# Four late weight blocks and the low-part copies placed elsewhere in the routing stage of a two-layer decoder trunk

## The reference

```
h = RMSNorm(x) * (1 + scale2) + shift2
q = (h @ w_q) -> (256 tokens, 8 heads, 2 halves, 128)
s1, s2 = q[:, :, 0] @ key1.T, q[:, :, 1] @ key2.T      # 128 scores each
v1, i1 = top_k(s1, 16); v2, i2 = top_k(s2, 16)
top, sel = top_k(v1[:, None] + v2[None, :], 16)        # of 256 candidates
expert = (i1, i2) at sel; gate = softmax(top)
out = sum over (head, k) of gate * gelu(h . u[expert]) * v[expert]
x = x + (1 + gate2) * out
```

## Time and profile before

| | us |
|---|---|
| median of three runs | 2905.32 |
| lowest, highest | 2900.86, 2907.9 |
| the profiled execution, as timed | 2900.86 |
| its span in the profile | 2899.1 |
| PE busy in it | 2784.7 |
| DVE busy in it | 2244.3 |
| ACT busy, POOL busy | 1164.6, 576.4 |
| mean granted clock of TensorE | 0.991 of 2.4 GHz |

### The profile page before, as it was taken

How to read it: one execution, slowest core, us unless ns; L and a number is a source line. 1 busy time by engine, 2 the same in 40 slices (tenths; PEclk the granted TensorE clock), 3 DMA queues, 4 the chain that set the end, 5 groups by cost and what they waited for, 6 DMA issues and landing times. The chain is left out here.

```text
span 2899.1 us, 49831 instructions
## 1 busy us (share of the span) xinstructions
PE 2784.7 (96%) x19146; PEld 2528.6 (87%) x19146; DVE 2244.3 (77%) x4294; ACT 1164.6 (40%) x1662; POOL 576.4 (20%) x354
## 2 busy tenths in 40 slices
PE   6999998899999999999999999889999999999998
PEld 6998887789999998877899987777999999977776
DVE  7998665569987658888889987655899776688887
ACT  4534421234454444333355342222444444433334
POOL 0000002101677730000000000021207777200000
PEclk9999999999999999999999999999999999999999
DMA  7553442255788778788645535341568787788885
GB/s 290 189 188 121 162 162 74 89 204 189 211 236 258 198 221 288 277 287 288 244 155 189 175 109 192 100 153 41 215 206 225 230 244 200 245 289 290 284 278 198
DMA packets 258979, 593.71 MB, mean 205 GB/s; under 512 B 82608, under 2 KB 198064, under 8 KB 200240
## 3 DMA queue, kind: packets, MB, share of 16 engines
q1 hardware_dynamic: 205456, 573.53, 57.2%
q0 software_dynamic: 36864, 0.15, 2.6%
q10 hardware_dynamic: 16416, 16.78, 1.7%
HBM read 537.27 MB, written 53.08 MB: 204 GB/s over the span
## 5 line engine op out<-in xcount | busy, mean ns | idle before, releaser
L1067 PE MATMUL ps<-h_hi,u_hi 128*128 128x256 f32 x2048 | 588.2, 287 | 7.0 <-DVE u_lo L1931 6.4
L1067 PE MATMUL ps<-h_lo,u_hi 128*128 128x256 f32 x2048 | 579.2, 283 | 0.0
L1067 PE MATMUL ps<-h_hi,u_lo 128*128 128x256 f32 x2048 | 579.1, 283 | 0.0
L2175 POOL DMA_INDIRECT gate_rows<-route x256 | 474.8, 1854 | 300.0 <-DVE route L2045 132.0
L1931 DVE TENSOR_TENSOR u_lo<-ring,u_hi 128x1024 fp32r<-128x1024 f32 x256 | 312.3, 1220 | 200.3 <-ACT u_hi L1364 179.1
L1067 PEld LDWEIGHTS ps<-h_hi,u_hi 128*128 128x128 f32 x2048 | 392.3, 192 | 11.8 <-DVE u_lo L1931 11.5
L1067 PEld LDWEIGHTS ps<-h_lo,u_hi 128*128 128x128 f32 x2048 | 392.7, 192 | 0.0
L1067 PEld LDWEIGHTS ps<-h_hi,u_lo 128*128 128x128 f32 x2048 | 392.3, 192 | 0.0
L1385 ACT ACTIVATE u_hi<-ring 128x1024 fp32r<-128x1024 f32 x192 | 203.9, 1062 | 323.6 <-PE ps L1088 323.6
L1938 DVE TENSOR_TENSOR u_lo<-ring,u_hi 128x1024 fp32r<-128x1024 f32 x192 | 234.9, 1224 | 51.1 <-ACT u_hi L1385 50.8
L1364 ACT ACTIVATE u_hi<-ring 128x1024 fp32r<-128x1024 f32 x256 | 269.6, 1053 | 0.0
(11 more groups left out here) (374 smaller groups left out, 5290.8 us busy)
## 6 DMA issues: line engine op xcount, KB each, us to landing
ring<-in_stream SPq DMA_DIRECT2D x456, 1024.0 KB, 7.6
act_rows<-region SPq DMA_DIRECT2D x256, 128.0 KB
gate_rows<-rstd ACTq DMA_DIRECT2D x2, 8192.0 KB, 26.2
region<-gate_rows SPq DMA_DIRECT2D x256, 64.0 KB, 3.9
region<-act_rows SPq DMA_DIRECT2D x128, 128.0 KB, 4.5
small_inverse<-act_rows SPq DMA_DIRECT2D x128, 128.0 KB, 4.2
gate_rows<-route POOLq DMA_INDIRECT x256
region<-in_c SPq DMA_DIRECT2D x7, 512.0 KB, 5.6
```

What stands on the lines that cost most here:

```text
L1067: ins = mm(ps[:, c % 4, 0:T], x, y[:, k, :], start=k == 0 and i == 0, stop=k == KD - 1 and i == 2)
L2175: gp.indirect_dma_start(gate_cells, bass.IndirectOffsetOnAxis(ap=gate_at[:, r:r + 1].bitcast(I32), axis=0), gate_weight[:, r:r + 1], None, ...
```

## The change

It moves work and computes the same.

- `GATE_AFTER` is (13, 15, 17, 19) and was (30, 33, 36, 39): the four late blocks of `W_ada` come behind the U blocks of chunks 27, 31, 35 and 39, and no longer behind those of chunks 61, 67, 73 and 79. `gate_ada(j)` moves with them, from the loop over one-hot steps into `between`: it follows the `u_low` of the block's second chunk at once.
- `LO_IN_HEAD[1]` is (0, 0, 0, 0, 0, 0, 0, 2) and was (0, 0, 0, 0, 0, 1, 2, 3): the selections of the first pass hold two copies, both in the last head, instead of six.
- So every later count falls by four: `TOP_AT` is (37, 0) for (41, 6), `ROUTE_AT` is 47 for 51 and `GATE_AT` is 50 for 54. The `u_low` copies that are no longer in the routing come behind it.
- `portion` rounds down: three copies in a selection come behind steps 3, 6 and 9, and came behind steps 2, 5 and 8.

```diff
-GATE_AFTER = (30, 33, 36, 39)
+GATE_AFTER = (13, 15, 17, 19)
...
-LO_IN_HEAD = ((3,) * 8, (0, 0, 0, 0, 0, 1, 2, 3))
+LO_IN_HEAD = ((3,) * 8, (0, 0, 0, 0, 0, 0, 0, 2))
 LO_IN_TAIL = 11
-TOP_AT = (sum(LO_IN_HEAD[0]) + sum(LO_IN_HEAD[1]) + LO_IN_TAIL, sum(LO_IN_HEAD[1]))
+TOP_AT = (sum(LO_IN_HEAD[0]) + sum(LO_IN_HEAD[1]) + LO_IN_TAIL, 0)
...
 def portion(n, i, parts):
 
-    def upto(k):
-        return (2 * n * k + parts) // (2 * parts)
-    return upto(i + 1) - upto(i)
+    return n * (i + 1) // parts - n * i // parts
...
                     for c in range(split, split + n):
                         u_low(c)
+                        if c in (2 * p + 1 for p in GATE_AFTER):
+                            gate_ada(GATE_AFTER.index(c // 2))
                     split += n
...
                     if c + 2 < CHUNKS:
                         u_low(c + 2)
-                    if c + 1 in (2 * p for p in GATE_AFTER):
-                        gate_ada(GATE_AFTER.index((c + 1) // 2))
```

## The result

The changed kernel takes 2939.39 us (median of 4 runs, 2938.31 to 2944.91); the kernel before took 2904.74 in the same comparison (4 runs, 2900.86 to 2907.90). The ratio is 1.0117, with a 95% interval of 1.0103 to 1.0132: about 34 us slower. The prediction said 2932 with a range of 2915 to 2943 and called it slower. The direction, the range and the mechanism held; the size was 7 us too small against this median. The profiled execution took 2942.32 us, with a span of 2940.5.

The account below looks back on a forecast made before the run. PE was taken to bound most stages, with DVE leading in the second pass. Layer 2's +14.6 and layer 1's +13.2 made +27.8 us: 2928.7 on the profiled execution, 2933.1 on the median; forecast 2932, range 2915 to 2943.

Parts of the forecast that it names:

- Step 1: Ahead of chunk 0: the first u_low copy comes late, so PE waits 9.5 us.
- Step 2: At chunk 0: PE resumes at half clock for 4.2 us, chunk 0 lasts 2.1 us longer, net cost 1.4 us.
- The prediction's last sentence: If the clock stays at 1.00 at chunk 0, 1.4 us fall away, but decode(1) and the second pass give most back.
- Step 3: decode(1), ahead of the second pass: takes 32.5 us instead of 33.8, leaving PE a lead of 0.6 us at chunk 13.
- Step 4: Second pass of selections: three gate_ada add 6.9 us on DVE; chunk 36 starts 13.8 us later in layer 2.
- step 5: decode(0), behind the second pass: gate_ada(3) and two small instructions cost 1.8 us in layer 2, 1.0 in layer 1.
- step 6: One-hot loop: taking out the four gate_ada saves 1.0 us in layer 2, nothing in layer 1.
- Hidden gate_ada: Second pass and decode(0): DVE's added work is covered, so +12 us in all, 2917; chance 0.13.
- late loads: W_ada blocks sharing the ring with U blocks delay stores, 11 us a layer on top, 2954; chance 0.10.
- no difference: Whole kernel: PE's late start is absorbed, leaving the time within 0.3% (8.7 us); chance 0.03.
- faster: End of the U pass: DVE's routing, not PE, sets it; up to 11 us less in two layers, 2894; chance 0.03.

Follow-up runs that it names:

- PE kept busy: The changed kernel with 72 matmuls added on PE ahead of chunk 0, their results unused; 2936.43 us, ratio 1.0094 to the kernel before.
- experiments on gate_ada: The kernel before with only the four late W_ada blocks and their gate_ada moved early (GATE_AFTER 13, 15, 17, 19); 2925.57 us, ratio 1.0056.
- DVE's time alone: The kernel before with eight unused product-and-sum instructions a layer on DVE behind the copies of chunks 27, 31, 35 and 39, no load moved; 2925.54 us, ratio 1.0053.
- the later runs of the kernel before: 45 runs of the unchanged kernel before, on the two chips of the follow-up experiments; medians 2909.80 and 2910.58 us.

## Why the prediction came out as it did

*Step 1, the first copy.* Forecast: 9.5 us of idle. Measured: 9.53 and 9.54. Chunk 0 starts 10.66 us behind the last key scores, forecast 10.4. The counting of selections in the timeline was enough for this.

*Step 2, half clock.* Right: the granted clock is 0.50 (1.2 GHz) at 2151.50 to 2155.50, and chunk 0 takes 2156.83 - 2151.54 = 5.29 us, 5.0 by the forecast. PE kept busy showed the net price. It was 1.9 and 2.0 us at chunk 1, for 1.4 forecast, and 0.7 and 2.1 at the end of the stretches. Their sum is the 2.8 forecast (twice 1.4), but the layers differ by 1.4 us, so that agreement is in part luck. The prediction's last sentence, that steps 3 and 4 give most of it back, did not come true by chunk 36: 1.7 and 1.4 us were left there.

*Step 3, decode(1).* This is the mis-sized term of layer 2. It starts 13.9 us behind the landmark, as forecast (13.8), but takes 2188.26 - 2154.78 = 33.5 us, not 32.5. I had credited one microsecond to table loads that moved out of it; that credit was not there, and the row of before (33.8) was the better value. PE's lead at chunk 13 was as small as forecast: the copy ended at 2191.2, PE started it at 2191.7.

*Step 4, the second pass.* Forecast: 69.7 + 6.9 = 76.6 us, measured 2265.16 - 2188.26 = 76.9. The waits behind chunks 27, 31 and 35 came as said, 2.0 to 2.1 us for 2.2, but for the third of layer 1 (0.67). At chunk 36 layer 2 was 124.4 us behind the landmark and had been 109.2 before: +15.2 for 13.8 forecast, of which 1.0 is step 3. Layer 1 gave +11.9 for 12.2. The argument that a PE that takes chunks as DVE delivers them has no slack, in spite of its higher busy share, is what the experiments on gate_ada and on DVE's time alone bear out.

*The Trainium skill's rule.* By the highest occupancy (the Trainium skill, Perfetto Trace Analysis, Identifying the Most-Contended Engine) PE was the bound of that pass, and the rival that follows from it was priced at 2917. The trace after and these two experiments speak against that use of it where two engines are both nearly full.

*Steps 5 and 6, behind chunk 36.* From chunk 36 to the V pass, before took 2520.60 - 2224.85 = 295.75 us, after 2562.20 - 2265.30 = 296.90: +1.2 in layer 2, where 1.8 - 1.0 = 0.8 was forecast, and in layer 1 +2.4 for 1.0. Chunk 47, the last of decode(0) in the changed kernel, tells the two steps apart. In layer 2 it starts at 2256.68 before and 2299.18 after, in layer 1 at 830.85 and at 848.65. Up to there the delay grows by 2.1 and 1.9 us: step 5 was too small, by little in layer 2 (1.8) and by 0.9 in layer 1, where I had charged 1.0. Behind it layer 2 wins 0.9 us, the 1.0 of step 6, and layer 1 loses 0.5. So the size of step 6 held in layer 2, by luck: the largest wait of before behind this chunk, 0.58 us at chunk 51, was one for a copy of decode(0) and not in the one-hot loop. "In the one-hot loop, no wait at all" was wrong: where the kernel before waits 0.47 us for `hot` at chunk 66, the one after waits 0.87 at chunk 54, with no gate_ada left in that loop. The chains of waits lead both back to a store of a gelu result: 8.45 us long before, and after

```profile
2310.26 7.11 DMA act_rows<-region
```

The store ends at 2317.37, and high part, copy and one-hot matrices follow it up to PE's start at 2321.66. Reading the wait before as one for gate_ada was a mistake.

*What no step had.* Behind two microseconds of idle the clock was lower in some places: 0.60 at 2266.00 and 0.57 at 802.00, 24 and 23 matmuls in 4 us in place of 35 or 36. Each costs 11 or 12 x 0.12 = 1.3 to 1.4 us at the spot. Behind it the next wait for DVE is shorter by about as much (0.67 us at 814.94 instead of 2.1), so little is left of it at the end.

*The sum.* Forecast 27.8, U stretches 30.7: 1.8 us short in layer 2 and 1.1 in layer 1. The terms that were too small are decode(1) of step 3 (33.5 us for 32.5, in layer 2) and decode(0) of step 5 (0.9 us, in layer 1). The remaining 4 us up to the difference of the medians (34.7, with an interval of about 30 to 38) can't be told from zero; against the later runs of the kernel before, with about 29 in all, nothing of them is left. One more lesson lies in the baseline: I counted layer 2's second pass from before's layer 2, which has no wait at chunk 22. Layer 1 of before has one (0.97 us), and so have both of the experiments on the second pass at the same chunk in layer 2, about 1.0 and 1.2 us. Before's layer 2 was a favourable sample.

*The rivals.* Hidden gate_ada fell (15.8 us for it alone), late loads fell (the same waits without them), no difference and faster fell with the result.

## What to carry to other kernels

Where two engines are both over 97% busy in a stretch, shares don't say which one leads; compare when the producer's instruction ends with when the consumer starts. If these are 0.05 us apart in a steady rhythm, nearly everything added to the producer there is paid: 9.2 us of gate_ada a layer made the stretches 9.0 and 9.5 us longer. Four copies fewer ahead of the stretch cost 9 us with their softmax; that two more gain is shown by the traces alone (3.7 us), since the softmax moved by itself gave 6 of the 8 us. And read a term's price from both layers and from more than one execution, since a wait of 1 us came and went between executions of the same code.

## What the runs showed of the hardware

TensorE's granted clock fell behind idle times of 2.06 and 2.10 us: it was 0.60 and 0.57 over 4 us that begin 0.7 and 1.0 us behind PE's restart, so part of them was at 1.2 GHz and the rest at 2.4. Behind others of 2.00 and 2.09 us in the same kernel it stayed at 1.00, and so it did behind all six of 1.98 to 2.10 us in the run with PE kept busy ahead of chunk 0. The length of the idle time alone doesn't tell which it will be. An idle time of 9.5 us was followed by 0.50 in both layers. With 72 matmuls in its place the clock was 1.00 over the U stretches, and these were 2.8 us shorter in the two layers together, although PE had 72 matmuls (8.9 us) more to do in each.

A table load of ACT took 1.28 us. Stores of gelu results of the same size (128 KB) took from 5.70 us to 8.45 us, and the long ones reached PE through ACT and DVE as waits of 0.47, 0.87 and 1.87 us.
